# Sample state products on stacked high and low halves in one single-pass matmul, conv taps copied by ScalarE, cache loaded one pair ahead, in a hybrid decoder layer

## The reference, cut to what matters

```python
# HGRN2, 16 heads, per sample (T = 4 tokens, one chunk)
S = (jnp.exp(G_last[:, :, 0])[..., None] * S
     + jnp.einsum('bhsd,bhsv->bhdv', k_ * jnp.exp(G_last - G), i_))
# gated delta net, 32 heads = 16 pairs
v_new = u - jnp.einsum('bhtd,bhdv->bhtv', w, S)
S = (jnp.exp(g_last)[..., None] * S
     + jnp.einsum('bhsd,bhsv->bhdv', k_ * jnp.exp(g_last - gam)[..., None], v_new))
# before the delta net: causal convolution of width 4 over q, k, v; its first rows come from cache_conv
conv = cw[0] * ucat[:, 0:T]
for j in range(1, CONV_W):
    conv = conv + cw[j] * ucat[:, j:j + T]
```

## Time and profile before

| | us |
|---|---|
| median of 3 runs | 3870.2 |
| lowest and highest | 3865.06, 3881.84 |
| the profiled execution: its own time | 3863.55 |
| the profiled execution: its span | 3862.0 |
| PE busy in it | 3640.9 (94%) |
| DVE busy | 2271.8 (59%) |
| ACT busy | 1803.5 (47%) |
| POOL busy | 871.7 (23%) |
| mean granted TensorE clock | 0.960 |

### The profile page before, as it was taken

The page is one execution under the profiler, slowest core; times in us unless marked ns, Lnnn a source line. Parts: engine busy times, 40 slices in busy tenths (PEclk is TensorE's granted clock), DMA queues, the critical chain, the costliest instruction groups (busy, mean ns, idle before and its releaser), DMA issues.

```text
span 3862.0 us, 79063 instructions
## 1 busy us (share of the span) xinstructions
PE 3640.9 (94%) x25307; PEld 3320.6 (86%) x25307; DVE 2271.8 (59%) x4443; ACT 1803.5 (47%) x3802; POOL 871.7 (23%) x1035
## 2 busy tenths in 40 slices
PE   9899999999899999989999999999895999999997
PEld 2599999998789888888898888897684999999996
DVE  2566666646665666666566666546667545555555
ACT  1344545455444444546444544455463444444443
POOL 1022222201244444440344554411100000000000
PEclk9999999999999999999999999999996999999998
DMA  8644545569633334338543333357883555555553
GB/s 287 189 143 137 149 140 147 140 198 278 172 95 97 100 106 116 95 101 261 156 118 95 99 97 95 96 160 241 244 251 88 159 161 161 161 161 160 162 160 113
DMA packets 887592, 587.96 MB, mean 152 GB/s; under 512 B 23602, under 2 KB 820244, under 8 KB 886932
## 3 DMA queue, kind: packets, MB, share of 16 engines
q1 hardware_dynamic: 861268, 510.50, 46.3%
q0 software_dynamic: 26240, 76.41, 6.5%
HBM read 545.83 MB, written 40.99 MB: 152 GB/s over the span
## 4 chain that ended last, share of the span: by engine, by line
PE 79%; DVE 7%; issue 4%; DMA 4%; ACT 3%; POOL 1%; DVEq 0%; SPq 0%; ACTq 0%; POOLq 0%
PE acc L574 20%; PE acc L576 18%; PE acc L575 18%; PE acc L547 3%; PE bank L764 2%; PE bank L778 2%; PE bank L801 2%; PE bank L781 2%; PE bank L816 1%; DVE wlo L1453 1%; ACT whi L988 1%; DMA raw<-in_w_ada 1%; DVE h_S L1607 1%; PE bank L586 1%; PE bank L587 1%
## 5 line engine op out<-in xcount | busy, mean ns | idle before, releaser
L1453 DVE TENSOR_TENSOR wlo<-raw,whi 128x512 fp32r<-128x512 f32 x1799 | 1266.3, 721 | 980.4 <-ACT whi L988 962.3
L988 ACT ACTIVATE whi<-raw 128x512 fp32r<-128x512 f32 x1799 | 1100.7, 629 | 986.8 <-PE acc L576 923.4
L574 PE MATMUL acc<-ahi,whi 128*128 128x288 f32 x4112 | 1305.1, 317 | 42.1 <-DVE alo L1948 16.2
L575 PE MATMUL acc<-alo,whi 128*128 128x288 f32 x4112 | 1234.4, 300 | 0.0
L576 PE MATMUL acc<-ahi,wlo 128*128 128x288 f32 x4112 | 1230.1, 299 | 0.0
L574 PEld LDWEIGHTS acc<-ahi,whi 128*128 128x128 f32 x4112 | 793.6, 193 | 66.3 <-issue 45.5
L575 PEld LDWEIGHTS acc<-alo,whi 128*128 128x128 f32 x4112 | 794.9, 193 | 13.2 <-issue 11.5
L576 PEld LDWEIGHTS acc<-ahi,wlo 128*128 128x128 f32 x4112 | 794.5, 193 | 0.0
L574 PE MATMUL acc<-ohi,whi 128*128 128x288 f32 x1792 | 538.3, 300 | 25.0 <-DVE olo L1984 9.7
L575 PE MATMUL acc<-olo,whi 128*128 128x288 f32 x1792 | 532.6, 297 | 0.0
L576 PE MATMUL acc<-ohi,wlo 128*128 128x288 f32 x1792 | 531.1, 296 | 0.0
(11 more groups left out here) (431 smaller groups left out, 4638.5 us busy)
## 6 DMA issues: line engine op xcount, KB each, us to landing
raw<-in_w_in SPq DMA_DIRECT2D x386, 512.0 KB, 4.1
raw<-in_w_ada SPq DMA_DIRECT2D x192, 512.0 KB, 4.7
raw<-in_w_up SPq DMA_DIRECT2D x128, 512.0 KB, 4.2
raw<-in_w_down SPq DMA_DIRECT2D x128, 512.0 KB, 3.8
raw<-in_w_out_gdn SPq DMA_DIRECT2D x64, 512.0 KB, 5.1
raw<-in_w_o SPq DMA_DIRECT2D x34, 512.0 KB, 5.1
raw<-in_w_out_hg SPq DMA_DIRECT2D x32, 512.0 KB, 5.3
g_S<-in_state_gdn POOLq DMA_DIRECT2D x32, 512.0 KB, 5.9
```

The source lines that it names most:

```text
L574: mm(bank[:, 0:T], whi[:, s, r, :], hi[:, kt, :], start=(kt == 0), stop=False, skip_group_check=True)
L575: mm(bank[:, 0:T], whi[:, s, r, :], lo[:, kt, :], start=False, stop=False, skip_group_check=True)
L988: f(whi[:, s], raw[:, r], ACT.Copy).then_inc(sg["hi_made"], 1)
L1453: tt_(wlo[:, s], raw[:, r], whi[:, s].bitcast(F32), SUB).then_inc(sg["lo_made"], 1)
```

## The change

The samples' state products become one matmul in `F32R`. The 128 rows of both operands are filled with four stacked copies of the 32 sample rows: the keys as high, high, low, low (`h_st[:, 0]`, `g_kst`), the values as high, low, high, low (`h_st[:, 1]`, `g_vst`); summed over the rows this is (high + low) by (high + low). The copies are made by repeating the source ahead of a transposition four times (`h_k4`, `h_i4`, `g_ck4`, `g_khi` used as `guT4`); the high halves by an ACT copy that rounds, the low ones by a DVE subtraction. In the same edit ACT copies the taps, `load_cache` stands earlier in POOL's list, and the transpositions of `g_qp` stand at `s` = 1 in place of 0. The diff, cut:

```diff
 # HGRN2
-                    turn(R[3][0:NS, 0:P], hX[:, 3, TP:T], ident[:, :])
-                    turn(R[3][0:NS, P:2 * P], hi_[:, TP:T], ident[:, :])
+                    turn(R[3][:, 0:P], hk4[:, :, :].rearrange("p g t -> p (g t)"), ident[:, :])
+                    turn(R[3][:, P:2 * P], hi4[:, :, :].rearrange("p g t -> p (g t)"), ident[:, :])
 # PE, s == 8
-                        last = mm(R[2 + a][:, :], htoks[:, 0, :], hiXs[:, 4 * a:4 * a + 4, :]...,
+                        last = mm(R[2 + a][:, :], hst[:, 0, :], hiXs[:, 4 * a:4 * a + 4, :]...,
 # ACT, s == 1 (and at 24: f(hi4, acc..., broadcast to 4, Copy))
-                    f(htoks[0:NS, :, :], R[3][0:NS, 0:2 * P]..., ACT.Copy).then_inc(sg["h_tok"], 1)
+                    f(hvs[0:NS, :], R[3][0:NS, P:2 * P], ACT.Copy)
+                    f(hst[:, :, :], R[3][:, 0:2 * P]..., ACT.Copy).then_inc(sg["h_tok"], 1)
 # DVE, s == 1
-                    tt_(hAT[0:NS, TP:T], R[4][0:NS, TP:T], smask[:, :], MUL).then_inc(sg["h_at"], 1)
+                    tt_(hAT[0:NS, TP:T], R[4][0:NS, TP:T], smask[:, :], MUL)
+                    dve.wait_ge(sg["h_tok"], n + 1)
+                    for rows_, k in ((slice(2 * NS, P), 0), (slice(NS, 2 * NS), 1), (slice(3 * NS, P), 1)):
+                        last = tt_(hst[rows_, k, :], R[3][rows_, k * P:(k + 1) * P], hst[rows_, k, :].bitcast(F32), SUB)
+                    last.then_inc(sg["h_at"], 1)
 # POOL (and in decayed: pt(hk4, hk, hE[:, 3], broadcast to 4, MUL))
-                pt(hiXs[0:NS, :, :], htoks[0:NS, 1, :]..., cm4..., MUL).then_inc(sg["h_spread"], 1)
+                pool.wait_ge(sg["h_at"], n + 1)
+                pt(hiXs[:, :, :], hst[:, 1, :]..., cm4..., MUL).then_inc(sg["h_spread"], 1)
 # delta net, PE
                 if s == 0:
-                    (transpositions of g_tq, g_tk, g_qp)
+                    (transpositions of g_tq, g_tk), then_inc(sg["g_qk_turned"], 1)
+                if s == 1:
+                    (waits for g_qp, g_tail_out, g_tokv; transpositions of g_qp), then_inc(sg["g_qk_turned"], 1)
                 if s == 2:
+                        mm(R[2 + a][:, 0:2 * P], m_incl...)
                         if a == 1:
                             pe.wait_ge(sg["g_qpt"], EARLIER + n + 1)
-                        mm(R[2 + a][:, 0:2 * P], m_incl...)
                 if s == 16:
-                        last = turn(R[5][0:NS, e * P:(e + 1) * P], guTs[:, e, :], ident[:, :])
+                        last = turn(R[5][:, e * P:(e + 1) * P], gkhi[:, e, :], ident[:, :])
 # PE, s in (20, 24)
-                        last = mm(R[4 + a][:, :], gkls[:, e, :], gvX[:, 4 * a:4 * a + 4, :]...,
+                        last = mm(R[4 + a][:, :], gkst[:, e, :], gvX[:, 4 * a:4 * a + 4, :]...,
 # ACT
+                if s == 5:
+                    (the three copies of the taps into gcw)
                 if s == 0:
-                    act.wait_ge(sg["g_qk_turned"], n + 1)
+                    act.wait_ge(sg["g_qk_turned"], 2 * n + 1)
                     f(gqT...), f(gkT...)
+                if s == 1:
+                    act.wait_ge(sg["g_qk_turned"], 2 * n + 2)
                     (copies to gqpT and gQW)
                 if s == 4:
+                    act.wait_ge(sg["g_tokv"], EARLIER + n + 1)
+                    f(gkhi[2 * NS:P].bitcast(F32R), gk32[2 * NS:P], ACT.Copy)
+                    f(gkst[0:2 * NS], gk32[0:2 * NS], ACT.Copy)
                     sigmoid_z(2 * n + 2)
                 if s == 17:
                     f(gvns[0:NS, :, :], R[5][0:NS, 0:2 * P]..., ACT.Copy)
+                    f(gvst.bitcast(F32R), R[5][:, 0:2 * P]..., ACT.Copy).then_inc(sg["g_vns"], 1)
 # DVE
                 if s == 5:
-                    (the three copies of the taps into gcw)
+                    tt_(gkst[2 * NS:P], gk32[2 * NS:P], gkhi[2 * NS:P], SUB)
                 if s == 21:
+                        tt_(gck4 (128 x 128), gca..., gce..., MUL)
                 if s == 44:
+                        last = ts(gk32[:, e, :], R[5][:, P:2 * P], gss[:, 2, 2, 1:2], gsc[:, e, 8:9], MUL, MUL)   # e = 0, 1
+                if s == 17:
+                    dve.wait_ge(sg["g_vns"], n + 1)
+                    for rows_ in (slice(NS, 2 * NS), slice(3 * NS, P)):
+                        last = tt_(gvst[rows_], R[5][rows_, 0:2 * P]..., gvst[rows_], SUB)
+                    last.then_inc(sg["g_vlo"], 1)
-                nc.vector.memset(gvX[rows_, :, :], 0.0)      # twice, ahead of the first pair
-                nc.vector.memset(gkls[rows_, :, :], 0.0)
 # POOL
-                scaled(gkls[0:NS], NS, 2, 8).then_inc(sg["g_tokd"], 1)
                 level(n, 3)
+                if cache:
+                    pool.wait_ge(sg["g_halo_turned"], n + 2)
+                    load_cache(n + 2)
                 level(n, 4)
...
-                pool.wait_ge(sg["g_vns"], n + 1)
+                pool.wait_ge(sg["g_vlo"], EARLIER + n + 1)
-                    pt(gvX[0:NS, :, :], gvns[0:NS, e, :]..., cm4..., MUL).then_inc(sg["g_vx"], 1)
+                    pt(gvX[:, :, :], gvst[:, e, :]..., cm4..., MUL).then_inc(sg["g_vx"], 1)
```

132 lines of the change are left out of this document (81 added, 51 removed).

## The result

The changed kernel takes 3897.0 us (median of 4 runs, 3885.2 to 3901.2) against 3867.7 for the kernel before on the same chip: a ratio of 1.0065, interval 1.0048 to 1.0083. Forecast were 3808 us, some 60 less; by the medians it came out 29 more. The profiled execution has a span of 3898.6 us, against 3862.0.

A forecast was written before the change was run, and what follows sets the result against it. PE, busy 94% of the span, was taken as the bound. The terms -60 - 12 - 2.4 + 11 + 2 gave -61.4 us from a median of 3870.2, so a forecast of 3808 us, range 3762 to 3842.

The forecast's parts named there:

- Products, -60: Sample state products in HGRN2 and delta net: single-pass F32R takes 1.25 us off PE for each of 48 heads.
- rival (3): Sample products: a pass with 128 stationary columns costs half the old product, not a quarter; -42, 3828 us; chance 0.07.
- Clock, 8 either way: Granted clock: falls behind the small products stay, only where they land may shift; 8 us either way.
- The first third of a pair, -12: Delta net, transpositions to small state products: of 4.82 us PE idle only about 0.75 a pair goes, over 16 pairs.
- (a): First third: scaled q's transpositions move to step 1; their wait goes, but what follows comes some 0.65 us later.
- (b): First third: earlier cache rows end the 1.56 us wait; level 0's masks come later, blocked by DVE, transposed at 1484.8.
- (c): First third: taps (4.32 us) leave DVE for ACT at no cost, which ends PE's wait of 1.77 us.
- New waits near step 20, +11: Later in a delta-net pair: a late spread or level-4 update costs 0.7 us a pair, between 0 and 1.7.
- HGRN2's spread, +2: HGRN2: the spread waits for one more ACT copy and three DVE subtractions; 0.1 us a head, between 0 and 0.8.
- Cleared buffers, -2.4: Ahead of the first delta-net pair: clears of g_vX and g_kls leave the chain PE waited 9.0 us for.
- Rival (2): Waits come back elsewhere: 0 at the pair's start, +27 at sample products, +13 in HGRN2; -22, 3848 us; chance 0.15.
- (1): Delta-net waits do go: masks never blocked, 2.5 us a pair, none new at sample products; -100, 3770 us; chance 0.2.

The follow-up runs named there:

- experiment 13: Changed kernel with HGRN2's small products spread, scaled q at step 0 and g_Ui/g_Us first, its stacked sample products read as F32: 3771.5 us, ratio 0.9748.
- experiment 1: Kernel before with only the HGRN2 part of the change (stacks, wider spread, single-pass products), delta net as before: 3863.5 us, ratio 0.9984.
- experiment 4: Changed kernel with five more single-pass products over 512 columns at step 20 of each HGRN2 head: 3888.4 us, ratio 1.0062.
- experiment 5: Changed kernel with two more single-pass products over 512 columns at step 20 of each HGRN2 head: 3884.2 us, ratio 1.0052.
- experiment 6: Changed kernel with transpositions and copies of the scaled q back at step 0: 3876.2 us, ratio 1.0015.
- experiment 10: Changed kernel with g_Ui and g_Us on DVE moved ahead of weight pieces, the gate and the keys' low half: 3806.8 us, ratio 0.985.
- experiment 7: Kernel before with only the taps copied by ACT and the cache rows loaded half a pair earlier: 3853.0 us, ratio 0.9967.
- experiment 12: Changed kernel with HGRN2's small products spread, scaled q at step 0, g_Ui/g_Us first, and slab 1's taps at step 16, not 18: 3734.0 us, ratio 0.9650.

## Why the prediction was wrong

By its own steps, in us, each with what the profile after and the experiments show:

- **Products, -60**: right in size. Their spacing is 0.23 us, as taken; two lines of PE's timeline, of which the first holds the two products:

```profile
453.42 1.02 PE L650 MATMUL bank<-h_iXs,h_st 128*128 128x512 f32 x2
454.28 0.29 PE L583 MATMUL acc<-ahi,whi 128*128 128x288 f32 x1
```

  The recorded start of the first overlaps the product ahead of it; the second starts at 454.05, 0.23 before the next instruction. Undisturbed a head saves 1.15 to 1.28 (35.01 us in F32 against 33.73, experiment 13) and a pair 2.5 (PE busy 79.35 in F32 against 76.80 in single pass, both at a clock of 0.98), 58 to 60 in all. The doubled price of rival (3) is out.
- **Clock, 8 either way**: this is the step that failed. It came to an estimated 57. The prediction said that the falls behind the small products "stay" and that only where they land may shift. The runs show two things in its place. In HGRN2 (38 us more at half clock in fifteen heads) each turn of the loop is the same, so a shorter turn moves every row of small products against the clock's changes in the same way, and 11 of 15 heads get the long fall (experiments 1, 4 and 5): it isn't a matter of chance that evens out. In the delta net (99 us more in fifteen pairs) the falls behind the row stayed as they were, and new ones came behind the waits of the first third (experiments 6 and 10); the prediction priced those waits without a fall behind them. No rival had either, and this term alone carries the result out of the range. Why a fall gets long, and why a wait is followed by one in some pairs only, stays open.
- **The first third of a pair, -12**: it came to +18 (waits at `g_qp`, `g_QW`, `g_levs`, `g_Us` and the cache: 68.9 before, 86.6 after). (a) was right: the wait of about 2 us ahead of `m_str` is there, 2.35, and the two waits for the scaled q grew from 21.8 to 33.3 us, 0.7 a pair as priced; only the fall behind it wasn't foreseen. (b) was right: the cache's wait is gone, the mask took 2.43 us and level 0 is waited for with 1.3 us a pair. (c) was wrong in the full change: the prediction said that the taps leave DVE and that this ends the wait of 1.77. It counted the duration of the operation that stood there, 4.32, and not what stands next in DVE's list while POOL still works. With the taps and the cache moved alone the wait did end (20.5 to 3.8 us, experiment 7); with the subtraction for the keys in DVE's list as well the piece behind it is held. The prediction even asked "what is late next?" for the masks and not for DVE. The wait for `g_Us` grew from 20.5 to 32.9.
- **New waits near step 20, +11**: 15.1, and by the mechanism named: the taps of slab 1 run beside the spread (three of them take 3.22 us, where three had taken 1.70), and the level-4 update is late. The spread itself isn't waited for. In experiment 12, with these taps two steps earlier, the wait fell to 9.4. The size, 11 against 15, is near.
- **HGRN2's spread, +2**: 0; its wait was 0.5 and is 0.6. By the Trainium skill ("SBUF — State Buffer", "Who interferes with whom") subtractions that read PSUM and one SBUF tile shouldn't contend with POOL; the trace agrees here: in one head the three took 0.90 us together (447.70) while POOL spread the prompt's values. It agrees too for the low half of the keys, which reads two: 1.38 us beside the masks, and 0.43 in experiment 6 at 1483.57, behind them. The gate ahead of it was held there in its place, for 3.33 us.
- **Cleared buffers, -2.4**: 9.0 to 6.3, -2.7.

The terms as measured give -60 + 57 + 18 + 15 - 3 = +27, and the spans differ by 36.6. Some 10 us are in none of them: no row was found for them. Rival (2), waits that come back elsewhere, was nearest: its sum was -22, and without the clock the measured terms give -30. But it put 13 us on HGRN2 and nothing on the pair's start, where the waits grew. Rivals (1), (3) and (4) don't hold.

## What to carry to other kernels

Where PE is the bound and the loop is short, ask of every saving what it does to the granted clock: look at how many turns of the loop have a fall and behind what, and price the case that each turn gets the next longer one; price a new wait with a fall behind it; better, break up the rows of small matmuls first, and save then. When an operation leaves an in-order engine at a place where another engine holds it, the next one that reads two SBUF tiles can take its place: put what others wait for ahead of all of them. The fastest versions here, 3.5% under the kernel before, have the change and such an order; the same orders without the stack give 2.4%, and the change without the order costs 0.7%.

## What the hardware showed that was not expected

- The clock falls though PE idled little: 0.52 us in the 18.87 up to the row's middle (444.13 to 463.00). In the stretch from 463.00 to 469.90 PE and its weight loads are both busy 6.90 of 6.90 us at a clock of 0.51. It begins within a row of fifteen products with 4 or 32 columns each, every one behind the load of 128 stationary columns. Broken up between weight products of 288 columns, and with the wait of 0.52 us gone, the same instructions leave the clock at 1.00 over 473 us of heads.
- In heads and pairs the falls were 3.4, 6.8 or 10.2 us long in the traces, at a cost of 1.3 us for the short and 2.9 for the middle one. Which of them a head got ran in a cycle of six or seven heads before and after the change and in experiments 1 and 4 (not in 5), and 1.15 us more work in each head made them shorter (half clock in the fifteen heads 82 to 55 us).
- In the changed kernel a wait of 2.35 us at step 2 had a fall at its end or right behind it in 13 of 16 pairs; with the waits there 0.65 and 1.07 us on average there was none, although PE waited no less over the whole stage (114 against 108 us). With the same 2.35 us, but shorter waits later in the pair (experiment 10), 6 of 16 pairs had it.
